# Expert jobs of a mixture-of-experts layer: from split reduced-precision products to native fp32, 64-slot jobs by row-tile pairs in the two column halves of the array, and expert 0's first 64 tokens as a 64-slot job ahead of all others

## The reference

```
def moe_swiglu(h, router, w1, w3, w2):
    logits = (h @ router).astype(F32)
    top_v, top_i = lax.top_k(logits, TOP_K)          # TOP_K = 2 of 8
    gates = jax.nn.softmax(top_v, axis=-1)
    dense_gate = jnp.sum(jax.nn.one_hot(top_i, N_EXPERTS) * gates[..., None], axis=-2)
    for e in range(N_EXPERTS):
        y = y + swiglu(h, w1[e], w3[e], w2[e]) * dense_gate[..., e:e + 1]
# swiglu(h, w1, w3, w2) = (silu(h @ w1) * (h @ w3)) @ w2, w1 and w3 1024 x 3584, w2 3584 x 1024
```

## Time and profile before

| | us |
|---|---|
| time, median of three | 1486.57 |
| span of the profiled execution (first to last instruction) | 1486.1 |
| PE busy | 1429.3 |
| DVE busy | 1135.2 |
| ACT busy | 927.7 |
| first weights of the expert layer asked for | 525.2 |
| first product of an expert job | 577.8 |
| last 2 MB of expert weights asked for | 1436.2 |

### The profile page before, as it was taken

How to read it: one execution, slowest core, us unless ns; L and a number is a source line. 1 busy time by engine, 2 the same in 40 slices (tenths; PEclk the granted TensorE clock), 3 DMA queues, 4 the chain that set the end, 5 groups by cost and what they waited for, 6 DMA issues and landing times.

```text
span 1486.1 us, 18710 instructions
## 1 busy us (share of the span) xinstructions
PE 1429.3 (96%) x7010; PEld 1135.0 (76%) x7010; DVE 1135.2 (76%) x1182; ACT 927.7 (62%) x969; POOL 79.7 (5%) x68
## 2 busy tenths in 40 slices
PE   7999999999999998999999999999999899899997
PEld 5777888888876886888888777778677678677675
DVE  1627377777363638988898899899898998998996
ACT  3243344444234235776877788888797897887885
POOL 0361000000036000000000000000000000000000
PEclk9999999999999999999999999999999999999998
DMA  9522616450833082999999899999999999999992
GB/s 322 203 92 86 240 43 212 171 213 1 293 130 102 12 329 110 357 366 334 336 373 362 341 405 412 411 416 410 413 412 408 416 418 406 418 419 407 412 419 80
DMA packets 120875, 435.09 MB, mean 293 GB/s; under 512 B 5727, under 2 KB 30453, under 8 KB 113653
## 3 DMA queue, kind: packets, MB, share of 16 engines
q1 hardware_dynamic: 120628, 433.83, 75.9%
q0 software_dynamic: 192, 0.53, 0.1%
HBM read 433.28 MB, written 1.05 MB: 292 GB/s over the span
## 4 chain that ended last, share of the span: by engine, by line
PE 64%; DVE 18%; issue 13%; ACT 4%; DMA 0%; DVEq 0%; SPq 0%; ACTq 0%
PE bank L2033 24%; DVE ring_lo L1462 12%; PE bank L1544 7%; PE bank L1931 5%; PE bank L1549 5%; PE bank L1567 4%; ACT w_hi L910 3%; PE bank L1935 3%; PE bank L2059 3%; PE bank L2041 2%; PE bank L1978 1%; PE bank L1530 1%; PE bank L1821 1%; PE bank L1822 1%; PE bank L1828 1%
## 5 line engine op out<-in xcount | busy, mean ns | idle before, releaser
L1462 DVE TENSOR_TENSOR ring_lo<-ring,w_hi 128x2048 fp32r<-128x2048 f32 (+1 forms) x350 | 728.9, 2123 | 72.7 <-ACT w_hi L910 71.8
L910 ACT ACTIVATE w_hi<-ring 128x2048 fp32r<-128x2048 f32 (+1 forms) x350 | 608.3, 1782 | 134.6 <-PE bank L2033 134.5
L2033 PE MATMUL bank<-w_hi,xg 128*128 128x512 f32 x1120 | 408.2, 395 | 6.2 <-DVE ring_lo L1462 4.9
L2033 PE MATMUL bank<-ring_lo,xg 128*128 128x512 f32 x896 | 360.1, 402 | 19.4 <-DVE ring_lo L1462 17.3
L2033 PEld LDWEIGHTS bank<-w_hi,xg 128*128 128x128 f32 x1120 | 211.3, 189 | 51.8 <-DVE ring_lo L1462 5.4
L2033 PEld LDWEIGHTS bank<-ring_lo,xg 128*128 128x128 f32 x896 | 168.5, 188 | 76.1 <-DVE ring_lo L1462 41.5
L2033 PE MATMUL bank<-ring_lo,at_hi 128*128 128x512 f32 x400 | 162.2, 405 | 5.9 <-DVE at_hi L1445 5.9
L2033 PE MATMUL bank<-w_hi,at_hi 128*128 128x512 f32 x400 | 157.5, 394 | 0.5 <-DVE at_lo L1447 0.5
L794 ACT ACTIVATE wf_hi<-ring 128x1024 fp32r<-128x1024 f32 x66 | 69.8, 1060 | 98.5 <-PE bank L1931 67.5
L1931 PE MATMUL bank<-x_both,wf_hi 128*128 128x512 f32 x336 | 118.8, 395 | 0.0
L2033 PEld LDWEIGHTS bank<-ring_lo,at_hi 128*128 128x128 f32 x400 | 75.1, 188 | 42.7 <-DVE ring_lo L1462 24.1
(11 more groups left out here) (358 smaller groups left out, 1640.3 us busy)
## 6 DMA issues: line engine op xcount, KB each, us to landing
ring<-in_moe_w SPq DMA_DIRECT2D x168, 2048.0 KB, 11.2
ring<-in_ffn_w SPq DMA_DIRECT2D x18, 1536.0 KB, 6.9
ring<-in_w_in SPq DMA_DIRECT2D x6, 2048.0 KB, 14.7
ring<-in_w_out SPq DMA_DIRECT2D x8, 1024.0 KB, 4.9
ring<-in_ffn_w SPq DMA_DIRECT2D x3, 2048.0 KB, 7.9
ring<-in_w_in SPq DMA_DIRECT2D x4, 1024.0 KB, 15.0
ring<-in_xa_wkv SPq DMA_DIRECT2D x2, 2048.0 KB, 15.0
ring<-in_w_in SPq DMA_DIRECT2D x2, 1184.0 KB, 6.4
```

Source lines behind the costliest of these rows:

```text
L910: act.activation(w_hi[:, i % NB, 0:cols.stop - cols.start], ring[:, slot_of(u), cols], ACT.Copy)\
L1462: dve.tensor_tensor(ring_lo[slot_of(u)][:, cols], ring[:, slot_of(u), cols], w_hi[:, i % NB, 0:cols.stop - cols.start], sub).then_inc(S["l ...
L2033: ins = mm(dst[:, :], st_, mv, start=opens, stop=closes, skip_group_check=small)
```

## The change

Both kinds of job use the weights as they land, in native fp32: the splitting by ACT and DVE, the buffers `w_hi` and the waits on them go. A full job has one native matmul per block of weights, with all 128 tokens. A 64-slot job has one native matmul per block too, with 64 stationary columns; the products of an even block of rows go to partitions 0 to 63 of the bank, those of the odd one to partitions 64 to 127, and the two halves are added later by the products that were there for hi and lo.

Expert 0's first 64 tokens are a 64-slot job of their own, written out ahead of the loops. It waits for no table: its slots are the first 64 ranks. If expert 0 has more than 64 tokens, the rest is a full job behind. The other experts get a full job if they have 64 or more tokens (`limit` 63). PE frees a ring slot once per transfer, with that transfer's last matmul, and the same count now tells ACT and DVE that rows are done.

```
-    put("limit", np.concatenate(([-1.0], np.full(N_EXP - 1, SMALL), np.full(N_EXP, P)))[None, :])
+    put("limit", np.concatenate(([SMALL], np.full(N_EXP - 1, SMALL - 1), [SMALL + P], np.full(N_EXP - 1, P)))[None, :])
...
-                def split(i):
-                    u, cols = job_cols(i % JOB_PIECES, small)
-                    dve.wait_ge(S["hi_ready"], pieces + (i + 1))
-                    dve.tensor_tensor(ring_lo[slot_of(u)][:, cols], ring[:, slot_of(u), cols],
-                                      w_hi[:, i % NB, 0:cols.stop - cols.start], sub).then_inc(S["lo_ready"], 1)
...
+            def small_job(j, last=False):
+                def products(w, d, part):
+                    u = UNIT_OF[w, d, part]
+                    s, width = slot_of(u), (2 if w == 2 else CHUNKS[d]) * FC
+                    n = 4096 // width
+                    pe.wait_ge(arrived[s], landed[u // RING])
+                    for x in range(0, n, 2):
+                        for half in range(width // FC):
+                            for side in range(2):
+                                k, at = n * part + x + side, (x + side) * width + FC * half
+                                if w == 2:
+                                    dst, rows = ps[6 + half], s_act[:, (HALF0[d] + part) % 4, x + side, :]
+                                    opens, closes = d == 0 and x == 0, d == NCH - 1 and part == 1 and x == n - 2
+                                else:
+                                    dst, rows = ps[w - 1 + half], xs[:, k, 0:SMALL]
+                                    opens, closes = k < 2, k >= KT - 2
+                                i = mm(dst[SMALL * side:SMALL * side + SMALL, :], rows, ring[:, s, at:at + FC],
+                                       start=opens, stop=closes)
+                    i.then_inc(slot_free[s], 1)
...
+            def full_job(j):
+                def products(w, d, part):
+                    pe.wait_ge(arrived[s], landed[u // RING])
+                    for x in range(n):
+                        for half in range(width // FC):
...
+                            i = mm(dst[:, :], rows, ring[:, s, at:at + FC], start=opens, stop=closes)
+                    i.then_inc(slot_free[s], 1)
...
+            keep_busy(4, 4)
+            small_job(0)
+            pe.wait_ge(S["jobs_ready"], 1)
...
+            with pe.Fori(1, n_full) as j:
+                full_job(j)
+            with pe.Fori(n_full, n_last) as j:
+                small_job(j)
+            small_job(n_last, True)
```

More of the change, by code:

```diff
@@ L40 @@
 HALVES = sum(CHUNKS)
[L41 to L43 removed]
+MAX_JOBS = N_EXP + 4
+NB = 4
 FPIECE = 1024
@@ L74, in slot_of, with job_turns, row_end, on @@
     return SLOTS[u % RING]
[L77 to L115, removed]
+def job_turns(j):
+    return [j * JOB_TURNS + (2 * LAYER_TURNS - 3 + t + 1) for t in range(JOB_TURNS)]
+def row_end(w, d):
+    u = UNIT_OF[w, d, CHUNKS[d] - 1]
+    return slot_of(u), u // RING
+def on(eng, x):
+    return x if isinstance(x, int) else eng.snap(x)
 NEG, MARK, HALF = -3.0e38, -3.4e38, -3.2e38
@@ L928, in job, with turned @@
[L928 to L937 removed]
+                def turned(d, x):
+                    act.wait_ge(S["j_tps"], hn[d][x])
+                    act.activation(f_act[:, (HALF0[d] + x) % 4, :, :], v3(ps[4 + x], 0, 512, 4), ACT.Copy)\
+                       .then_inc(S["j_t"], 1)
@@ new lines, in full_job @@
+                act.wait_ge(S["j_gps"], j1)
+                for b in range(2):
+                    i = act.activation(xs[:, 4 * b:4 * b + 4, :], v3(ps[2 + b], 0, 512, 4), ACT.Copy)
+                i.then_inc(S["j_gh"], 1)
+                for half in range(2):
+                    yrow_out(j, half)
+                for d in range(NCH):
+                    rows1(d)
+                    for x in halves(d - 1) if d else ():
+                        turned(d - 1, x)
+                    if d == 0:
+                        this_job(j)
@@ L938, in _ @@
+                for x in halves(NCH - 1):
+                    turned(NCH - 1, x)
+                hot_turned(j1)
+            with act.Fori(1, n_full) as j:
+                full_job(j)
             with act.Fori(n_full, n_last) as j:
-                job(j, True)
-            job(n_last, True, True)
+                small_job(j)
+            small_job(n_last)
             for half in range(2):
@@ L1479, in job @@
-                turns(JOB_PIECES)
-                if not last:
-                    for i in range(AHEAD):
-                        split(JOB_PIECES + i)
-                    gather_lo(j2)
-            with dve.Fori(0, n_full) as j:
-                job(j, False)
+                for half in range(2):
+                    yrow_out(j, half)
+                rows3(0)
+                for t in range(TT):
+                    combined(j, t)
+                next_slots(dve.snap(j + 1))
+                for d in range(1, NCH):
+                    rows3(d)
@@ new lines, in small_job @@
+                turned_hot()
+                for part in range(2):
+                    if not last:
+                        gather(j2, part)
+                    pe.wait_ge(S["j_t"], hn[NCH - 1][part])
+                    products(2, NCH - 1, part)
+            keep_busy(4, 4)
+            small_job(0)
+            pe.wait_ge(S["jobs_ready"], 1)
+            n_jobs = pe.value_load(tabi[0:1, 0:1], min_val=N_EXP, max_val=MAX_JOBS)
+            n_full = pe.value_load(tabi[0:1, 1:2], min_val=2, max_val=MAX_JOBS - 2)
@@ L2072, in job @@
                         pe.wait_ge(S["j_cv"], j * 2 + 1)
[L2073 to L2080 removed]
+                    for x in range(CHUNKS[d - 1]):
+                        turn(d - 1, x)
+                    rows_of(3, d)
                     if d == 1:
```

426 lines of the change are left out of this document (172 added, 254 removed).

## The result

The changed kernel takes 1451.35 us (median of four runs, 1451.11 to 1451.60), the kernel before 1487.70 (four runs, 1486.51 to 1489.10). The ratio is 0.9757, 95% interval 0.9743 to 0.9771. The profiled execution took 1451.60 us, its span is 1449.5.

What follows compares the result with a forecast made beforehand. PE bounds the first two jobs, weight transfers the rest: start 576.4, jobs 92.0 and 152.9, table 1.0, landing 830.2, 119 transfers to 1434.7, last products and 12.6 behind, plus 0.5: 1451.4 us, range 1445 to 1480.

Steps and rivals of the forecast that it cites:

- Price of a pair: PE, 64-slot jobs: two native 512-column products to the two partition halves cost 0.858 us together; without overlap 1.716.
- Rival A: PE's pairs lose overlap: each pass shows a 0.14 us weight load, a pair costs 1.14 us, total 1549 us; chance 0.09.
- the 0.045 extra in rows 9: Earlier trace, two-half matmuls: second records start 0.26 us later against 0.215 alone; counted as a burst's start, not a rate.
- Start of job 0: PE begins expert 0's 64-slot job at 576.4 us instead of 577.8; first ring slot freed at 579.8 instead of 590.0.
- The table's 1.0 us: PE reads the table of jobs between expert 0's job and the full job, costing 1.0 us.
- Jobs: PE time: 92.0 us for a 64-slot job, 152.9 for the full job, so expert 3's costs 28 us more.
- Transfers: Weight DMAs at a floor of 413 GB/s, 5.08 us each; a 64-slot job's 21 take 106.6 us.
- The lag: PE's last product ends 3.6 us behind the last landing instead of 22.9, with the split gone; 12.6 more to the end.
- step 5: After the full job, 119 transfers of 5.08 us run to 1434.7; PE catches up within two jobs, then waits harmlessly.
- Rival B: Hand-over waits between PE, ACT and DVE replace the splits, keeping 64-slot jobs at 106.7 us: 1487 us; chance 0.04.
- the milder form: 1 us waits at each of some ten engine hand-overs in the first two jobs: 1460 to 1483 us; chance 0.10.
- Rival C: Expert 0 has over 64 tokens, so nine jobs run: 106.6 us more, 1558 us; chance 0.02.

Runs made afterwards that it cites:

- the kernel with one half: Changed kernel with both blocks of each pair in 64-slot jobs sent to partitions 0 to 63, so no overlap: 1890.45 us, ratio 1.2701 to the kernel before.
- the split full job: Changed kernel with the one full job back on split fp32r products, 64-slot jobs still in native pairs: 1424.44 us, ratio 0.9576 to the kernel before.
- half the transfers of w2: Changed kernel with half of each 2 MB w2 transfer left out in all jobs but the first: 1386.56 us, ratio 0.9318 to the kernel before.
- the ballast: Changed kernel plus 45 useless PE products, about 10 us: in each of five looped 64-slot jobs 1451.83 us; once, in the first job alone, 1461.64 us.
- The order by fours: Changed kernel with each transfer's four lower-half products first, then its four upper-half ones: 1486.29 us, ratio 0.9988 to the kernel before.
- the order by twos: Changed kernel with the partition halves alternating after every two products: 1455.15 us, ratio 0.9778 to the kernel before.

## Why the prediction was right

**Price of a pair.** Predicted c = 0.858, two streams in full. Measured: passes of both halves 0.429 apart (577.024 and 577.453, the other half 5 and 6 ns behind; 5 to 8 in most of the kernel, 35 to 37 in one pass of seven), and a PE-bound job of 92.4 against 92.0, so c = (92.4 - 19.9) / 84 = 0.863 if all the rest is as counted. Rival A's 1.14 and the 1.04 read from the earlier trace rows are out. That the 0.045 extra in rows 9 were the start of a burst fits: in the first row of job 0 the lower half's first two passes are 0.48 apart (575.684, 576.165) and the later ones 0.429. The first rival without any overlap was worked out at 1888, and the kernel with one half took 1890.45.

**Start of job 0.** Predicted 576.4, was 575.7; the first slot freed at 579.8, was 579.4. The table's 1.0 us between job 0 and the full job isn't there: the last transfer's products of job 0 start at 664.68 and run 3.65 us, and the full job's first starts at 668.27. This term was wrong by its whole size, and small; in the kernel that reads the table ahead of job 0, PE is idle there for 0.28.

**Jobs.** 92.0 and 152.9, were 92.6 and 153.1; the full job's end 822.3, was 821.4. The +28 us for expert 3's job are the price that the split full job gives back: 26.9 measured.

**Transfers.** The one that the full job's last product sets free was to land at 830.2 and landed at 829.6; then 119 at 5.08 us to 1434.7, were 119 at 5.08 to 1433.7. That a job stands on this floor was read from 413 GB/s in the jobs and 408 in a stretch where DVE and ACT were called nearly idle. They are not: in 530 to 560 us DVE is busy for 11.0 of 30 us, ACT for 12.1 and PE for 29.2, so that stretch shows no more than a lighter load on two engines. (Nor is DVE over 90% busy in all expert jobs, as I wrote ahead of the prediction: in the two full ones it is 86 and 87%.) The conclusion holds all the same. In the changed kernel DVE is busy for 7.4 us of a looped job and the rate is still 413, and half the transfers of w2 and the ballast show what it binds. The estimate from the Trainium skill's "DMA: Bandwidth & Descriptors", "Bandwidth", 1434 us for the whole, doesn't hold here: the rate stays at 413 to 414 in the jobs.

**The lag.** 3.6 us behind the last landing, was 3.8; 12.6 to the end, was 12.0. The size is right; the reason given for the old 22.9, that the split stands between a landing and its products, isn't needed. The order by fours splits nothing, and yet its last product ends 20.1 us behind the last landing (1452.12 to 1472.27). With half of w2's transfers it is 24.9, with one half alone 48.4. The kernels whose jobs end up waiting for transfers all have 3.8 or 3.9, among them the order by twos and the split full job. In all these the lag is a backlog of landed transfers: it stays when a job takes PE as long as its transfers or longer (106.4 against 106.6 us by fours), and the changed kernel works it off, since 92.4 is 14 less. For the kernel before this is the likely reading too. The prediction has this too, in its first section and its step 5. How much of the 22.9 was the splitting's own delay, no run tells.

**The sum.** The span came out at 1449.5 for 1450.9. Around it I put 0.5, from the median of one set of runs and the span of another; the profiled execution's own time is 2.1 over its span. The two errors, -1.4 and +1.6, have opposite signs, so that the forecast of 1451.4 meets the median of 1451.35 is in part luck.

**Rival B** had waits within a job. In the PE-bound stretches PE is busy for the whole length (92.40 of 92.40), and from 576 to 828 us it isn't seen to wait for ACT or DVE at all, so the milder form is out too. **Rival C**, nine jobs: 168 transfers are eight.

**What the prediction didn't split.** The last landing moved by 16.9 us. Nearly all of it is PE's first two jobs. In the kernel before the third job's first product is this one:

```profile
836.39 0.39 PE L2033 MATMUL bank<-ring_lo,xg 128*128 128x512 f32 x1
```

After, it starts at 821.38: 15.0 earlier, of which 2.1 are the earlier start of job 0 and 12.9 that 92.6 + 153.1 = 245.7 us replace 258.6. Behind it the transfers are in a row in both kernels; the other 2 us are gaps between the first of them before the change (landings at 844.2 and 850.2 us are 6.0 apart, those at 875.6 and 881.8 are 6.2, where 5.1 is the rule). What made them, no run tested.

## What to carry to other kernels

Find the job or stage where the transfers wait for the engine, and save engine time there: here 28 us of PE time in the one full job were worth 27 us, and 50 us in the looped jobs nothing. A job that takes the engine just as long as its transfers keeps the backlog that it starts with, and the backlog is paid behind the last landing. Two 64-column products into the two partition halves of a bank cost as much as one, if they stand next to each other (or two apart) in the program; four of one side and then four of the other lose what the change gained. A precision scheme can be chosen for each kind of job: half-full jobs by native pairs, full ones by split fp32r (three times 0.23 us against twice 0.43).

## What the runs showed of the hardware

- PE starts products of the other column half ahead of earlier ones in the program: by fours the upper half's first starts four passes, 1.77 us, behind the lower half's, and across two transfers records of the later one (`s_act`, 916.63) start before records of the earlier (`xs`, 917.06). By twos the upper half starts at once. Both orders have three unstarted passes skipped. The Trainium skill, "TensorE: Matmul & The Clock Gate", Part 3, "The mechanism", has matmuls start and end in strict program order; these rows don't.
- With the two halves in turn, the second follows the first by 5 to 8 ns in six of seven passes of the changed kernel (1008 of 1176), and by 35 to 37 ns in the rest, and each pass takes 0.429 us of the array with or without the other half.
- A 64-column load of 0.14 us is hidden under a running matmul even in the same rows and the same columns of the array: passes 0.43 apart in the kernel with one half. The Trainium skill, "TensorE: Matmul & The Clock Gate", Part 3, "The mechanism", has a line that lets loads overlap only where the row groups differ, and these rows disagree with it. The same section also names a background weight buffer into which a load can be pulled ahead; that would fit, and no run here tells what hides the load.
- More transfers in the queue (24.9 us from issue to landing instead of 12.2) leave the rate at 413 GB/s.
